# One RWKV-7 mixer layer: pairs' coupling work moved in between the receptance slots, key slots fed two at a time, filler products in the norm's hole

## The chip, the cores and the metric

One Trainium2 chip, one core. The metric is device time of one launch in microseconds, the median of several runs. The kernel runs five engines with queues of their own: TensorE (PE, with weight loads PEld), VectorE (DVE), ScalarE (ACT), GpSimd (POOL) and SyncE (SP, which issues all DMAs here). Each takes its instructions in order and waits at semaphores.

## The reference

One inference step of a 2-layer decoder with d = 1024, for 16 meta + 256 prompt tokens and 8 sequences of 8 new tokens (336 rows together). Each layer is: half an FFN, a token mixer, half an FFN. Layer 0 mixes with RWKV-7 (16 heads of 64), layer 1 with a short gated convolution. The mixer of layer 0, cut to what matters:

```python
xr, xw, xk, xv, xa, xg = [h + xx * mu[c] for c in range(6)]   # xx = previous row - h
r, k, v = xr @ w_rkv[0], xk @ w_rkv[1], xv @ w_rkv[2]
w = -softplus(-(w0 + tanh(xw @ w1) @ w2)) - 0.5
decay = exp(-exp(w))
a = sigmoid(a0 + (xa @ a1) @ a2)
g = sigmoid(xg @ g1) @ g2
kk = k * k_k;  kk = kk / max(norm(kk, per head), 1e-12)
k = k * (1 + (a - 1) * k_a);  b = kk * a
def step(S, inp):
    S = S * d_t + einsum(S, -kk_t) * b_t + v_t * k_t
    return S, einsum(S, r_t)
```

All matrix products are made of three passes of rounded parts (high x high, high x low, low x high), so every weight and every activation is split into a high part (ScalarE) and a low part (VectorE).

## The kernel before, in words

**Weights** come in slots of 1 MB into `raw[0]` and `raw[1]` in turn. `split_act` (L246) writes `w_hi` on ScalarE, `split_dve` (L251) writes `w_lo` on VectorE, and TensorE's use of a slot waits for that. A buffer pair is split anew only when TensorE has ended the slot two earlier. `mix_sp` issues the loads; `load_mix(k)` waits for the split two slots earlier. The stores of z (`couplings`) and their loading back into `gt` follow in the same SP queue.

**The mixer** (`mix_pe`, `mix_act`, `mix_dve`) works on slots in the order: key (0 to 3), decay LoRA (4), a LoRA (5), receptance (6 to 9), gate (10), value (11 to 14), gate out (15). `project` (L811) makes two output tiles of 128 rows per slot, 8 input tiles x 2 x 3 passes = 48 matmuls; a slot with `fresh` waits for each input tile `x_lo` as it arrives. `lora_inner` is L823, `lora_out` L837. Each group of results has PSUM banks given by `BANKS`, and `open_group` waits until these are free.

**The head norm.** ScalarE squares kk, TensorE sums (L846), VectorE takes a max (L1450), ScalarE a root (L1222), VectorE a reciprocal (L1453), and `spread` (L859) spreads the result for each pair of heads.

**The pairs.** For the 8 pairs of heads, VectorE runs `pair_front` (L1546 scan of the log decays, L1549 norm, L1551 and L1553 factors), `pair_back` (L1562, L1566 decays on a, b and k) and `r_decayed` (L1406, which reads the receptance from PSUM). ScalarE makes the exponentials (L1175, L1176, L1184) and, after all pairs, the ends (L1231). TensorE then makes for each pair the couplings (L897, 44 small products), the turned b and k (L883, 44) and the sum for the bonus (L874). VectorE masks the couplings into z (L1492) and makes the product for the sum (L1480); ScalarE keeps the turned rows (L1242, L1243).

**Order written by hand.** Before, TensorE runs two spreads ahead of each receptance slot, and all couplings after the four slots. VectorE runs all fronts and backs first, then a loop over pairs with rk product, `low(XG, p)`, `mixed(XG, p + 4)` and z. After that come the gate slot (10), the value slots, VectorE's triangular inverses (from L1363) and a chain over chunks.

Of the kernel before, what the change touches and what calls it, by code (L numbers as in the profile page):

```python
# [32 lines left out]
P = 128  # L33
# [44 lines left out]
def build_program(nc, x_dram, vec_dram, const_dram, shift_dram, conv_dram, wkv_dram, gu_dram, down_dram,  # L78
                  mix_dram, wo_dram, scin_dram, scout_dram, blockeye_dram, y_out, wkvp_out, wkvs_out, shift_out,
                  convo_out, zt_dram, tt_dram):  # L80
    with ExitStack() as ctx:
# [257 lines left out]

        def ffn_pe(pe, f):  # L340
# [278 lines left out]
        BANKS.update({R_GROUP + i: b for i, b in enumerate((0, 2, 6, 0))})  # L619
# [3 lines left out]
        Z_BANKS = (4, 6)  # L623

        MIXED = {XK: (4, 5, 4, 5), XR: (4, 5, 4, 5), XG: (4, 5, 2, 3), XV: (4, 5, 2, 3)}
# [151 lines left out]
        def mix_pe(pe):  # L777
# [3 lines left out]
            def open_group():  # L781
# [3 lines left out]
                if 2 <= g < R_GROUP + 2:  # L785
                    pe.wait_ge(mix_evac, g - 1)
                elif g == R_GROUP + 3:
                    pe.wait_ge(r_scaled, 2)
                elif g == G_GROUP:
                    pe.wait_ge(kv_turned, PAIRS)  # L790
                elif g == V_GROUP:
                    pe.wait_ge(rk_kept, 1)
                elif V_GROUP < g < GATE_GROUP:
                    pe.wait_ge(mix_evac, g - 5)
                elif g == GATE_GROUP:
                    pe.wait_ge(z_ready, 14)
                elif g > GATE_GROUP:
                    pe.wait_ge(mix_evac, g - 6)
                return BANKS[g]

            def project(slot, ver, fresh, final=False, shift=0):
# [4 lines left out]
                for k in range(KT):  # L806
# [6 lines left out]
                    if final and k < KT - 1:  # L813
                        last.then_inc(x_used, 1)
                last.then_inc(mix_out, 1)
# [25 lines left out]
            for s in range(4):  # L841
                project(s, XK, s == 0, s == 3, PAD)
# [24 lines left out]

            pe.wait_ge(a_normed, PAIRS)

            def sum_rk(p):  # L870
                pe.wait_ge(rk_ready, p + 1)
                if p == 0:
                    pe.wait_ge(r_scaled, PAIRS)
                pe.matmul(PS[0:HEADS, 0, :T], con[:, K_SEL + 16 * p:K_SEL + 16 * p + 16], tmp[p % 2][:, RD],  # L874
                          start=(p == 0), stop=(p == PAIRS - 1)).then_inc(rk_sum, 1)

            def turn_bk(p):
                if p:
                    pe.wait_ge(kv_turned, p)
                for c in range(CHUNKS):  # L880
                    for hh in range(2):
                        rows = slice(HD * hh, HD * hh + HD)
                        last = pe.matmul(PS[rows, 2 + c // 8, (c % 8) * HD:(c % 8 + 1) * HD],  # L883
# [4 lines left out]
            for p in range(PAIRS):  # L888
                pe.wait_ge(a_scaled, p + 1)
                pe.wait_ge(bk_scaled, p + 1)  # L890
                pe.wait_ge(r_scaled, max(p + 1, 6 if p else 1))
                if p >= 2:
                    pe.wait_ge(z_ready, 2 * p - 2)
                for c in range(CHUNKS):
                    for hh in range(2):
                        rows = slice(HD * hh, HD * hh + HD)
                        last = pe.matmul(PS[rows, Z_BANKS[p % 2] + c // 8, (c % 8) * 64:(c % 8) * 64 + 64],  # L897
# [3 lines left out]
                if p >= 1:  # L901
                    turn_bk(p - 1)
                if p >= 2:
                    sum_rk(p - 2)
            turn_bk(PAIRS - 1)
            sum_rk(PAIRS - 2)
            sum_rk(PAIRS - 1)
# [210 lines left out]
        def mix_act(act):  # L1118
# [58 lines left out]

            def decay_r(p):
# [31 lines left out]
            act.activation(thi[:, 1, :], tmp[1][:, :T], ACT.Copy).then_inc(lora_hi, 1)  # L1210
            for s in range(4):
                x_hi_tile(XR, 2 + s)
                evac(6 + s, [(sw[:, m, PAD:], ACT.Sigmoid, vec[:, m, V_W0:V_W0 + 1], False) for m in (2 * s, 2 * s + 1)])
            split(6)
            x_hi_tile(XR, KT - 2)
            x_hi_tile(XR, KT - 1)
            for s in range(4):
                evac(10 + s, [(bk[:, m, :, 0, :], ACT.Sigmoid, vec[:, m, V_A0:V_A0 + 1], True) for m in (2 * s, 2 * s + 1)])
                factors(s)
                if s == 1:  # L1220
                    act.wait_ge(kk_max, 1)
                    act.activation(tmp[3][0:HEADS, :T], tmp[3][0:HEADS, :T], ACT.Sqrt).then_inc(kk_root, 1)  # L1222
            split(7)
            for p in range(PAIRS):
                if p in (2, 4, 6):
                    split(7 + p // 2)
                decay(p)
                if p >= 1:
                    decay_r(p - 1)
# [573 lines left out]
```

## Time and profile before

| | us |
|---|---|
| median of 3 runs | 1461.81 (1461.13 to 1462.18) |
| the profiled execution | 1460.54 |
| its span, first to last instruction | 1458.8 |
| TensorE busy in the span | 1392.3 (95%) |
| VectorE busy | 857.1 (59%) |
| ScalarE busy | 584.8 (40%) |
| mean granted TensorE clock | 0.973 |

The mixer of layer 0 lies between about 266 and 570 us of the span; the part in which the change edits anything ends at about 434. Positions in the rows are microseconds from the start of the span. A row of the timeline merges instructions of one kind that follow each other; its duration is from the first start to the last end, and neighbouring instructions overlap a little, so costs are better read from start to start.

### The profile page before, as it was taken

The numbers are of one execution on the slowest core, as the hardware profiler recorded it, in microseconds if no ns is written. First come the engines' busy times: TensorE is split into PE (matmuls) and PEld (weight loads), VectorE is DVE, ScalarE is ACT, GpSimd is POOL, SyncE is SP. The second block draws the span as 40 slices with busy tenths as digits, with TensorE's granted clock in tenths as the row PEclk, the third lists the DMA queues.
The fourth block names the chain that finished last, engine by engine and source line by source line (L and its number), as shares of the span: only waits on it lengthen the run. The fifth ranks groups of instructions, "written<-read, shape, count | busy, mean of one in ns | idle before, by whom it ended". The sixth has DMA issues, their size and how long they took to land.

```text
span 1458.8 us, 28480 instructions
## 1 busy us (share of the span) xinstructions
PE 1392.3 (95%) x11742; PEld 1350.0 (93%) x11742; DVE 857.1 (59%) x1294; ACT 584.8 (40%) x757; POOL 14.0 (1%) x28
## 2 busy tenths in 40 slices
PE   5999999698799998999999999999999999999997
PEld 5999999686689986899999999999999999999997
DVE  4555544776869366665555555555456867555543
ACT  5333333477344333353333344333333235333332
POOL 0000000300000000000000000000000000000000
PEclk9999999898799899899999999999999999999999
DMA  5333334232125211144443454443444444444342
GB/s 224 130 140 137 135 128 148 103 118 87 59 71 170 73 42 62 58 145 144 144 146 131 145 180 146 145 144 117 148 167 145 145 145 145 144 148 156 126 145 98
DMA packets 44220, 188.98 MB, mean 130 GB/s; under 512 B 15888, under 2 KB 17296, under 8 KB 28016
## 3 DMA queue, kind: packets, MB, share of 16 engines
q1 hardware_dynamic: 44144, 187.89, 37.5%
q8 instruction: 57, 0.93, 0.3%
q14 instruction: 19, 0.16, 0.0%
HBM read 182.65 MB, written 5.22 MB: 129 GB/s over the span
## 4 chain that ended last, share of the span: by engine, by line
PE 90%; DVE 4%; ACT 3%; issue 2%; POOL 1%; DMA 1%; SPq 0%; ACTq 0%; DVEq 0%
PE psum L335 48%; PE psum L367 22%; PE psum L811 5%; PE psum L505 4%; ACT w_hi L246 1%; PE psum L1046 1%; PE psum L997 1%; PE psum L972 1%; PE psum L883 1%; PE psum L1066 1%; DMA w_raw<-in_gu 1%; PE psum L1030 1%; PE psum L897 1%; PE psum L1015 1%; PE psum L1079 1%
## 5 line engine op out<-in xcount | busy, mean ns | idle before, releaser
L251 DVE TENSOR_TENSOR w_lo<-w_raw,w_hi 128x2048 fp32r<-128x2048 f32 (+1 forms) x188 | 388.4, 2066 | 238.4 <-ACT w_hi L246 238.0
L335 PE MATMUL psum<-x_hi,w_hi 128*128 128x322 f32 (+2 forms) x1600 | 499.9, 312 | 19.1 <-DVE x_lo L298 17.5
L246 ACT ACTIVATE w_hi<-w_raw 128x2048 fp32r<-128x2048 f32 (+1 forms) x188 | 326.0, 1734 | 459.0 <-PE psum L335 227.0
L335 PE MATMUL psum<-x_hi,w_lo 128*128 128x322 f32 (+2 forms) x1600 | 500.6, 313 | 0.0
L335 PE MATMUL psum<-x_lo,w_hi 128*128 128x322 f32 (+2 forms) x1600 | 500.5, 313 | 0.0
L335 PEld LDWEIGHTS psum<-x_hi,w_hi 128*128 128x128 f32 x1600 | 303.8, 190 | 20.7 <-issue 17.3
L335 PEld LDWEIGHTS psum<-x_hi,w_lo 128*128 128x128 f32 x1600 | 302.7, 189 | 0.0
L335 PEld LDWEIGHTS psum<-x_lo,w_hi 128*128 128x128 f32 x1600 | 301.8, 189 | 0.3
L367 PE MATMUL psum<-h_hi,w_lo 128*128 128x322 f32 (+2 forms) x704 | 219.8, 312 | 0.0
L367 PE MATMUL psum<-h_lo,w_hi 128*128 128x322 f32 (+2 forms) x704 | 219.2, 311 | 0.0
L367 PE MATMUL psum<-h_hi,w_hi 128*128 128x322 f32 (+2 forms) x704 | 218.8, 311 | 0.0
L367 PEld LDWEIGHTS psum<-h_hi,w_hi 128*128 128x128 f32 x704 | 133.3, 189 | 0.0
L367 PEld LDWEIGHTS psum<-h_hi,w_lo 128*128 128x128 f32 x704 | 132.8, 189 | 0.0
L367 PEld LDWEIGHTS psum<-h_lo,w_hi 128*128 128x128 f32 x704 | 132.5, 188 | 0.0
L390 ACT ACTIVATE h_hi<-tmp 128x322 f32 (+5 forms) x88 | 41.9, 476 | 205.9 <-DVE tmp L434 205.9
L428 DVE TENSOR_TENSOR tmp<-psum,rstd 128x322 f32<-128x322 f32 (+2 forms) x88 | 43.7, 497 | 111.5 <-PE psum L335 106.5
L436 DVE TENSOR_TENSOR h_lo<-tmp,h_hi 128x322 f32 (+5 forms) x88 | 43.8, 498 | 63.8 <-ACT h_hi L390 63.8
L811 PE MATMUL psum<-x_hi,w_hi 128*128 128x336 f32 x208 | 70.4, 339 | 10.5 <-DVE x_lo L1391 10.5
L811 PE MATMUL psum<-x_lo,w_hi 128*128 128x336 f32 x208 | 68.8, 331 | 0.0
L811 PE MATMUL psum<-x_hi,w_lo 128*128 128x336 f32 x208 | 68.5, 329 | 0.0
L278 DVE SCALAR_TENSOR_TENSOR x<-psum,x 128x322 f32<-128x322 f32 (+5 forms) x48 | 23.7, 494 | 72.1 <-PE psum L367 62.3
L811 PEld LDWEIGHTS psum<-x_hi,w_hi 128*128 128x128 f32 x208 | 41.6, 200 | 15.3 <-issue 12.9
(206 smaller groups left out, 1366.1 us busy)
## 6 DMA issues: line engine op xcount, KB each, us to landing
w_raw<-in_gu SPq DMA_DIRECT2D x88, 1024.0 KB, 4.8
w_raw<-in_down SPq DMA_DIRECT2D x64, 704.0 KB, 4.1
w_raw<-in_mix SPq DMA_DIRECT2D x16, 1024.0 KB, 4.8
w_raw<-in_scin SPq DMA_DIRECT2D x12, 1024.0 KB, 4.7
w_raw<-in_wo SPq DMA_DIRECT2D x4, 1024.0 KB, 4.8
w_raw<-in_scout SPq DMA_DIRECT2D x4, 1024.0 KB, 4.8
s<-in_wkv SPq DMA_DIRECT2D x8, 256.0 KB, 3.4
out_wkvs<-s SPq DMA_DIRECT2D x8, 256.0 KB, 2.0
```

Of the source, the lines that this page charges most:

```text
L246: act.activation(whi[par][:, :tiles * P], raw[par][:, :tiles * P], ACT.Copy).then_inc(hi_ready, 1)
L251: dve.tensor_tensor(wlo[par][:, :n], raw[par][:, :n], whi[par][:, :n].bitcast(F32), ALU.subtract).then_inc(lo_ready, 1)
L278: dve.scalar_tensor_tensor(out=x[:, m, c:], in0=ps[:, :T - c], scalar=alpha, in1=x[:, m, c:], op0=ALU.mult, op1=ALU.add).then_inc(x_new, 1)
L335: last = pe.matmul(PS[:, banks[j], :n], w[:, (2 * k + j) * P:(2 * k + j + 1) * P], v[:, k, :n], start=(k == 0 and i == 0), stop=(k == KT - ...
L367: last = pe.matmul(PS[:, 4 + par, :n], w[:, k * P:(k + 1) * P], v[:, kk, :n], start=(kk == 0 and i == 0), stop=(kk == FT - 1 and i == 2))
L390: act.activation(hhi[:, bass.ds(s, 1), :n], tmp[3][:, :n], ACT.Copy).then_inc(hhi_ready, 1)
L428: dve.tensor_tensor(tmp[0][:, :n], PS[:, 2 * par, :n], rstd[:, :n], ALU.mult).then_inc(gate_scaled, 1)
L436: dve.tensor_tensor(hlo[:, bass.ds(s, 1), :n], tmp[3][:, :n], hhi[:, bass.ds(s, 1), :n].bitcast(F32), ALU.subtract).then_inc(hlo_ready, 1)
L505: last = pe.matmul(PS[:, banks[j], :n], w[:, (2 * k + j) * P:(2 * k + j + 1) * P], v[:, k, :n], start=(k == 0 and i == 0), stop=(k == KT - ...
L811: last = pe.matmul(PS[:, b + j, shift:shift + T], w[:, (2 * k + j) * P:(2 * k + j + 1) * P], v[:, k, :], start=(k == 0 and i == 0), stop=( ...
L883: last = pe.matmul(PS[rows, 2 + c // 8, (c % 8) * HD:(c % 8 + 1) * HD], bk[rows, p, c, :, :].rearrange("p h t -> p (h t)"), con[rows, K_EY ...
L897: last = pe.matmul(PS[rows, Z_BANKS[p % 2] + c // 8, (c % 8) * 64:(c % 8) * 64 + 64], bk[rows, p, c, :, :].rearrange("p h t -> p (h t)"), ...
```

## The change

It does the following:

1. After the norm's own product, TensorE issues nine products of constants, 512 columns, into bank 7 (`warm`).
2. Key slots 0 and 1 run together: tile k of slot 0 when it arrives, and tile k - 3 of slot 1 (`pe_tile`).
3. Max, root and reciprocal of the head norm come earlier on VectorE and ScalarE; the banks of the LoRA groups and of the receptance change, and with them the waits in `open_group`.
4. The spreads 2 to 7 stand between the tiles of slot 6; VectorE's norm of a (`a_norm`) is a loop of its own ahead of the pairs.
5. Couplings 0 and 1 and the first sum stand between slots 8 and 9 on TensorE, the other couplings, sums and turns after slot 9 in a new order. VectorE takes z and the rk product inside the loop of pairs. Slot 8 waits for `r_scaled` 2, slot 9 for `r_scaled` 4.
6. ScalarE makes the ends per pair, and does `split(8)`, `(9)`, `(10)` at pairs 1, 3, 5; VectorE too.
7. Gate mixtures use other buffers, and all `low(XG, p)` come after the last z.

```diff
+        def warm(pe, bank, count):
+            for _ in range(count):
+                pe.matmul(PS[:, bank, :], con[:, K_BLOCK:K_BLOCK + P], con[:, 0:512], start=True, stop=True)
+        def pe_tile(pe, par, banks, k, n, xh, xl, shift=0):
+            ...  # the six matmuls of one input tile, as in project
-        BANKS.update({R_GROUP + i: b for i, b in enumerate((0, 2, 6, 0))})
+        BANKS.update({6 + i: b for i, b in enumerate((4, 6, 0, 2, 6, 4, 0, 2))})
+        BANKS.update({R_GROUP + i: b for i, b in enumerate((6, 0, 6, 0))})
-        Z_BANKS = (4, 6)
+        Z_BANKS = (2, 2, 2, 2, 2, 2, 2, 0)
...
-                if 2 <= g < R_GROUP + 2:
+                if 2 <= g < 6:
                     pe.wait_ge(mix_evac, g - 1)
-                elif g == R_GROUP + 3:
-                    pe.wait_ge(r_scaled, 2)
+                elif g == 7:
+                    pe.wait_ge(kk_max, 1)
+                elif 8 <= g < R_GROUP + 2:
+                    pe.wait_ge(mix_evac, (5, 6, 8, 7, 9, 10, 11, 13)[g - 8])
+                elif R_GROUP + 2 <= g < G_GROUP:
+                    pe.wait_ge(r_scaled, 2 * (g - R_GROUP - 1))
                 elif g == G_GROUP:
+                    pe.wait_ge(z_ready, 16)
                     pe.wait_ge(kv_turned, PAIRS)
...
-            for s in range(4):
-                project(s, XK, s == 0, s == 3, PAD)
+            warm(pe, 7, 9)
+            pe_slot_wait(pe, MIXB)
+            banks = [open_group(), open_group()]
+            for step in range(KT + 3):
+                if step < KT:
+                    pe.wait_ge(xlo_ready, 8 * XK + step + 1)
+                    last = pe_tile(pe, 0, (banks[0], banks[0] + 1), step, T, xhi, xlo, PAD)
+                    if step == KT - 1:
+                        last.then_inc(mix_out, 1)
+                if step == 3:
+                    pe_slot_wait(pe, MIXB + 1)
+                if step >= 3:
+                    last = pe_tile(pe, 1, (banks[1], banks[1] + 1), step - 3, T, xhi, xlo, PAD)
+            last.then_inc(mix_out, 1)
+            for s in range(2, 4):
+                project(s, XK, False, s == 3, PAD)
...
+                elif p == 0:                      # in spread(p)
+                    pe.wait_ge(kk_inv, 1)
+                    pe.wait_ge(mix_evac, 12)
-            pe.wait_ge(kk_inv, 1)
-            for s in range(4):
-                spread(2 * s)
-                spread(2 * s + 1)
-                project(6 + s, XR, s == 0, s == 3)
...
+            def couplings(p):
                 pe.wait_ge(a_scaled, p + 1)
                 pe.wait_ge(bk_scaled, p + 1)
-                pe.wait_ge(r_scaled, max(p + 1, 6 if p else 1))
-                if p >= 2:
-                    pe.wait_ge(z_ready, 2 * p - 2)
+                pe.wait_ge(r_scaled, p + 1)
+                if p == 0:
+                    pe.wait_ge(mix_evac, 14)
+                elif p < PAIRS - 1:
+                    pe.wait_ge(z_ready, 2 * p)
+                else:
+                    pe.wait_ge(r_scaled, PAIRS)
...
+            spread(0)
+            spread(1)
+            project(6, XR, True, between=lambda k: spread(k + 2) if k + 2 < PAIRS else None)
+            project(7, XR, False)
+            project(8, XR, False)
+            couplings(0)
+            couplings(1)
+            sum_rk(0)
+            project(9, XR, False, True)
+            couplings(2)
+            sum_rk(1)
+            couplings(3)
+            sum_rk(2)
+            couplings(4)
+            sum_rk(3)
+            turn_bk(0)
+            couplings(5)
+            sum_rk(4)
+            turn_bk(1)
+            turn_bk(2)
+            couplings(6)
+            sum_rk(5)
+            turn_bk(3)
+            turn_bk(4)
+            couplings(7)
+            sum_rk(6)
+            turn_bk(5)
+            turn_bk(6)
+            sum_rk(7)
+            turn_bk(7)
...
             for p in range(PAIRS):                # ScalarE
-                if p in (2, 4, 6):
-                    split(7 + p // 2)
+                if p in (1, 3, 5):
+                    split(8 + p // 2)
                 decay(p)
-                if p >= 1:
-                    decay_r(p - 1)
+                ends(p)
+                decay_r(p)
+            for p in range(3):
+                keep_bk(p)
             x_hi_tile(XG, 0)
             x_hi_tile(XG, 1)
             split(11)
+            keep_bk(3)
+            keep_bk(4)
+            for p in range(5, PAIRS):
+                x_hi_tile(XG, p - 3)
+                keep_bk(p)
...
+            for p in range(PAIRS):                # VectorE
+                a_norm(p)
+                if p == 4:
+                    split(7)
+            dve.wait_ge(mix_evac, 10)
+            dve.wait_ge(bk_padded, 1)
+            for p in range(PAIRS):
+                if p in (1, 3, 5):
+                    split(8 + p // 2)
+                pair_front(dve, p)
+                if p >= 1:
+                    pair_back(dve, p - 1)
+                    r_decayed(p - 1)
+                if p >= 2:
+                    take_z(p - 2)
+                    take_rk(p - 2)
+            pair_back(dve, PAIRS - 1)
+            r_decayed(PAIRS - 1)
+            take_z(PAIRS - 2)
+            take_rk(PAIRS - 2)
+            dve.wait_ge(a_scaled, PAIRS)
+            mixed(XG, 0)
+            mixed(XG, 1)
+            take_z(PAIRS - 1)
+            take_rk(PAIRS - 1)
+            split(11)
+            dve.wait_ge(rk_sum, PAIRS - 1)
+            mixed(XG, 2)
+            dve.wait_ge(rk_sum, PAIRS)
+            mixed(XG, 3)
+            for p in range(PAIRS):
                 low(XG, p)
                 if p + 4 < KT:
                     mixed(XG, p + 4)
```

`take_z(p)` waits for couplings(p) and for the ends of pair p, `take_rk(p)` for the scaled rows of pair p and for the sum two pairs back. `keep_bk(p)` is L1242 and L1243 with their waits. The max and the reciprocal of the head norm move from behind the x_lo tiles of the receptance to ahead of them (max) and to tile 3 (reciprocal); ScalarE's root moves from between the second and third sigmoid group of slot 5 to ahead of the first of slot 4.

## Rows read from the trace of the kernel before

**Rows 1.** The page: its first line and its first section.
```profile
span 1458.8 us, 28480 instructions
PE 1392.3 (95%) x11742; PEld 1350.0 (93%) x11742; DVE 857.1 (59%) x1294; ACT 584.8 (40%) x757; POOL 14.0 (1%) x28
```
**Rows 2.** Windows: stretch, length, busy time of each engine, PEclk, DMA share, GB/s.
```profile
276.60:283.00 6.40, 6.38 (x23) 5.72 (x24) 6.40 (x11) 1.45 (x3) 6.40 (x10) 0.55 0.01 3
...
388.00:400.00 12.00, 7.57 (x132) 7.22 (x132) 11.40 (x24) 5.76 (x11) 0.00 (x0) 0.57 0.01 3
400.00:425.00 25.00, 23.91 (x587) 19.54 (x588) 15.68 (x34) 7.60 (x19) 0.00 (x0) 0.93 0.31 70
```
**Rows 3.** Timeline, key slot 0 on TensorE: start, us, engine, line, operation.
```profile
276.62 0.62 PE L811 MATMUL psum<-x_hi,w_hi 128*128 128x336 f32 x1 [9.55 <-DVE x_lo L1391]
277.03 0.48 PE L811 MATMUL psum<-x_lo,w_hi 128*128 128x336 f32 x1
277.31 0.48 PE L811 MATMUL psum<-x_hi,w_lo 128*128 128x336 f32 x1
...
282.47 0.32 PE L811 MATMUL psum<-x_lo,w_hi 128*128 128x336 f32 x1
```
**Rows 4.** Timeline, VectorE, key tiles and the split behind them.
```profile
275.98 0.49 DVE L1391 TENSOR_TENSOR x_lo<-tmp,x_hi 128x336 fp32r<-128x336 f32 x1
...
277.84 0.49 DVE L1391 TENSOR_TENSOR x_lo<-tmp,x_hi 128x336 fp32r<-128x336 f32 x1
...
286.09 1.14 DVE L1391 TENSOR_TENSOR x_lo<-tmp,x_hi 128x336 fp32r<-128x336 f32 x2
...
291.59 2.29 DVE L251 TENSOR_TENSOR w_lo<-w_raw,w_hi 128x2048 fp32r<-128x2048 f32 x1
```
**Rows 5.** Timeline, ScalarE and VectorE around the root of the head norm.
```profile
335.14 0.98 ACT L1147 ACTIVATE bk<-psum,vec 128x352 f32<-128x352 f32 x2
...
337.42 1.28 ACT L1222 ACT_TABLE_LOAD   x1
...
339.23 2.24 DVE L1453 RECIPROCAL rstd<-tmp 16x336 f32<-16x336 f32 x1 [2.98 <-ACT tmp L1222]
```
**Rows 6.** The chain that ended last, in order of time: start, us, what.
```profile
341.52 2.60 PE psum L859 x4
344.12 9.00 PE psum L811 x48
...
425.72 37.13 PE psum L811 x240
```
**Rows 7.** Timeline, VectorE, pair 2 from its scan to the next pair's.
```profile
358.31 0.85 DVE L1546 TENSOR_TENSOR_SCAN sw<-con,sw 128x336 f32<-128x336 f32 x1
359.20 0.51 DVE L1549 TENSOR_TENSOR ar<-psum,ar 128x336 f32<-128x336 f32 x1
359.62 0.52 DVE L1551 TENSOR_TENSOR bk<-bk,fac 128x352 f32<-128x352 f32 x1
...
360.49 0.62 DVE L1562 TENSOR_TENSOR ar<-ar,tmp 128x15 f32<-128x15 f32 x3
...
361.83 0.85 DVE L1546 TENSOR_TENSOR_SCAN sw<-con,sw 128x336 f32<-128x336 f32 x1
```
**Rows 8.** Timeline, all engines, z and rk of a pair, then one round of the tail.
```profile
399.76 0.95 DVE L1492 TENSOR_TENSOR z<-psum,con 128x512 f32<-128x512 f32 x2
400.63 0.58 DVE L1480 SCALAR_TENSOR_TENSOR tmp<-ar,vec,bk 128x352 f32<-128x352 f32 x1
...
409.13 1.50 PE L897 MATMUL psum<-ar,bk 64*64 64x64 f32 x44
...
410.47 1.45 PE L883 MATMUL psum<-con,bk 64*64 64x64 f32 x44
...
411.85 0.74 PE L874 MATMUL psum<-tmp,con 128*16 128x336 f32 x2
411.96 0.60 ACT L1242 ACTIVATE bk<-psum 128x512 f32<-128x512 f32 x1 [2.19 <-PE psum L883]
```

More of the change, by code:

```diff
@@ L337, in pe_pair @@
             last.then_inc(out_sem, 1)
+        def warm(pe, bank, count):
+            for _ in range(count):
+                pe.matmul(PS[:, bank, :], con[:, K_BLOCK:K_BLOCK + P], con[:, 0:512], start=True, stop=True)
+        def pe_tile(pe, par, banks, k, n, xh, xl, shift=0):
+            for j in range(2):
+                for i, (w, v) in enumerate(passes(whi[par], wlo[par], xh, xl)):
+                    last = pe.matmul(PS[:, banks[j], shift:shift + n], w[:, (2 * k + j) * P:(2 * k + j + 1) * P], v[:, k, :n],
+                                     start=(k == 0 and i == 0), stop=(k == KT - 1 and i == 2))
+            return last
         def ffn_pe(pe, f):
@@ L814, in project @@
                         last.then_inc(x_used, 1)
+                    if between and k < KT - 1:
+                        between(k)
                 last.then_inc(mix_out, 1)
@@ L879, in turn_bk @@
                     pe.wait_ge(kv_turned, p)
+                else:
+                    pe.wait_ge(r_scaled, 6)
                 for c in range(CHUNKS):
@@ L882, in turn_bk @@
                         rows = slice(HD * hh, HD * hh + HD)
-                        last = pe.matmul(PS[rows, 2 + c // 8, (c % 8) * HD:(c % 8 + 1) * HD],
+                        last = pe.matmul(PS[rows, 6 + c // 8, (c % 8) * HD:(c % 8 + 1) * HD],
                                          bk[rows, p, c, :, :].rearrange("p h t -> p (h t)"),
@@ L896, in mix_pe @@
                         rows = slice(HD * hh, HD * hh + HD)
-                        last = pe.matmul(PS[rows, Z_BANKS[p % 2] + c // 8, (c % 8) * 64:(c % 8) * 64 + 64],
+                        last = pe.matmul(PS[rows, Z_BANKS[p] + c // 8, (c % 8) * 64:(c % 8) * 64 + 64],
                                          bk[rows, p, c, :, :].rearrange("p h t -> p (h t)"),
@@ L1454, in mix_dve @@
-            split(7)
-            dve.wait_ge(mix_evac, 14)
-            dve.wait_ge(bk_padded, 1)
-            for p in range(PAIRS):
-                if p in (2, 4, 6):
-                    split(7 + p // 2)
-                pair_front(dve, p)
-                if p:
-                    pair_back(dve, p - 1)
-                if p >= 3:
-                    r_decayed(p - 3)
-            pair_back(dve, PAIRS - 1)
-            dve.wait_ge(a_scaled, PAIRS)
-            r_decayed(PAIRS - 3)
-            for k in range(4):
-                mixed(XG, k)
-                if k % 2:
-                    r_decayed(PAIRS - 2 + k // 2)
@@ L1472, in mix_dve, with a_norm, take_z @@
-            split(11)
-            for p in range(PAIRS):
+            def a_norm(p):
+                dve.wait_ge(kk_spread, p + 1)
+                dve.tensor_tensor(ar[:, 0, p, PAD:], PS[:, 4 + p % 2, :T], ar[:, 0, p, PAD:], ALU.mult).then_inc(a_normed, 1)
+            def take_z(p):
+                dve.wait_ge(z_done, p + 1)
+                dve.wait_ge(ends_ready, 2 * p + 2)
+                for i, (c0, c1) in enumerate(((0, 8), (8, CHUNKS))):
+                    n = (c1 - c0) * 2 * C
+                    dve.tensor_tensor(z[:, :, p, c0:c1, :].rearrange("p h c t -> p c h t"),
+                                      PS[:, Z_BANKS[p] + i, :n].rearrange("p (c h t) -> p c h t", h=2, t=C),
+                                      con[:, K_ZMASK + c0 * 2 * C:K_ZMASK + c1 * 2 * C]
+                                      .rearrange("p (c h t) -> p c h t", h=2, t=C), ALU.mult).then_inc(z_ready, 1)
```

78 lines of the change are left out of this document (30 added, 48 removed).

## The prediction

> **What bounds the kernel now.** The first thing read is the page's head: one core, a span of 1458.8 us [rows 1]. All times below are positions in that profiled execution. The change touches only the mixer of layer 0, so the second view is the chain that ended last, in order of time. From 425.72 it is one unbroken stretch of TensorE work, 240 matmuls in 37.13 us (the G slot and the four V slots; 0.155 us a matmul, so 7.4 us a slot of 48) [rows 6]. TensorE goes on almost without a hole after that. What comes behind the start of the G slot is not edited, so the change is worth what it does to that one start, 425.72.
>
> Ahead of it, the windows and the timeline show TensorE waiting often, with its clock at half (1.2 GHz) for long parts: 0.55 granted in 276.6 to 283, 0.57 in 388 to 400 [rows 2]. The hole of the norm is 9.55 us long [rows 3]. In the pairs' stretch VectorE is the busiest (11.40 of 12 us in 388 to 400); in 400 to 425 TensorE is busy 23.91 of 25 [rows 2]. So before, VectorE does the eight pairs first, and then TensorE runs couplings, turns and sums pair by pair.
>
> **The change, part 1: the filler in the norm's hole.** Nine products of 512 columns with plain f32 operands. No row has this shape. Two f32 products of 336 columns took 2.60 us at half clock [rows 6], so 1.3 each with the drain, 0.65 at full clock, and 512/336 times that is 1.0: nine are 9 us, from 267.1 to 276.1, before the first key tile starts at 276.62 [rows 3]. At half clock they would take 17.8 us and end at 284.9; that bound costs 5.6 us below. TensorE was at full clock as the hole began, so I take the first.
>
> What does it buy? The first matmuls after the hole repeat every 0.28 us, and from 282.47 a matmul takes 0.32 from start to end, at full clock [rows 3]. But a tile of six at half clock is 1.7 us, and tiles arrive every 1.87 (275.98, 277.84) [rows 4], so half speed is hidden by VectorE. The row says 0 for the filler. The Trainium skill (TensorE: Matmul & The Clock Gate, Why this matters for your kernels) advises to warm TensorE up with matmuls ahead of the work. By that rule the forecast would be 1480.6; it stands among the rivals.
>
> **Part 2: two key slots per arriving tile.** Tile 7 of x_lo is ready at 287.2 (286.09 + 1.14) [rows 4]. Three tiles of slot 0 are done by 282.1; then 13 tiles remain (5 of slot 0, 8 of slot 1) at 0.93, so both end at 294.1. Before, slot 0 ends at 288.8 and slot 1 at 296.2: 2.1 us saved. But slot 0 now ends at 290.5, and its end frees the buffer for the split of slot 2: ScalarE 1.9, then VectorE 2.2 (2.29 recorded [rows 4]), ready at 294.8. So 0.7 goes back into a wait, and **1.4 us** remain. At the filler's bad bound the 16 tiles run from 284.9 to 299.8 instead.
>
> **Part 3: the root moved ahead.** Before, ScalarE does the square root between two pairs of sigmoids: a table load of 1.28 from 337.42, the root of 0.5 (VectorE starts behind it at 339.23), a table load again, then VectorE's reciprocal of 2.24, and at 341.52 the first spread [rows 5, 6]. After, the root stands ahead of all sigmoids (one load of 1.28 less in all), and the reciprocal is inside the receptance's x_lo loop, off the end. The spread now waits for bank 4, for the evacuation of group 11, which ended at 336.12 before (335.14 + 0.98) [rows 5]. From there: -1.4 (part 2), +1.8 (root and its load now ahead of it), +1.2 (ScalarE waits for receptance tile 5, which stands behind the reciprocal on VectorE), +0.5 (tiles 6 and 7 ahead of split 6): 338.2. The receptance starts **3.3 us earlier**.
>
> **Part 4: spreads between tiles.** The same eight spreads, six of them now inside slot 6. TensorE starts at half clock as before (slot 6 took 9.00 instead of 7.4 [rows 6]). Walking tile by tile, slot 6 with all spreads ends at 353.15, slot 7 at 360.55. VectorE is only free of the last spread at 352.0, since a_norm(p) can only follow spread p.
>
> **Part 5: the pairs, where the time is decided.** VectorE's costs from start to start [rows 7]: split 2.2; pair_front without the norm 1.75 (scan 0.89, then 360.49 - 359.62 = 0.87); pair_back 1.34 (361.83 - 360.49); r_decayed 0.42, taken from the norm of a, which also multiplies 128x336 out of PSUM (359.62 - 359.20). A z pair is 0.88, an rk product 0.50 [rows 8]. Two new waits bind them:
> - slot 8 uses the banks of slot 6 and waits for r_scaled 2; slot 9 uses those of slot 7 and waits for r_scaled 4;
> - VectorE goes on from r_decayed(1) straight into take_z(0), whose couplings stand behind slot 8 on TensorE; and from r_decayed(3) into take_z(2), behind slot 9.
>
> So each slot waits for VectorE, and VectorE waits for each slot; queued behind that wait are splits 9 and 10 and all later pairs. From 352.0: front 0 to 353.75; ScalarE does three exponentials, two small ones and split 8 by 356.85; VectorE's split to 359.05; two fronts, two backs, two r (7.0) to 366.05. TensorE idles 5.5 us; slot 8 runs to 373.45 and couplings 0 (1.5) to 374.95: **8.9 us of idle VectorE**. Then z, rk, split 9, front, back, r, z, rk, front, back, r: 2 x 1.38 + 2.2 + 2 x 3.51 = 12.0, to 386.95. Slot 9 ends at 394.35 (385.8 before), with VectorE idle 8.9 again.
>
> The tail begins there (S). Before, it was paced by TensorE at 3.38 a pair: couplings at 409.13, turn at 410.47, sum at 411.85 (1.34, 1.38, 0.66) [rows 8]. After, couplings 1 to 6 share one bank pair, so each waits for the z before it. The chain: VectorE from S+1.5 to the factor product of pair 7 is 3 x 1.38 + 2.2 + 2 x 3.51 + 1.31, S+16.2; ScalarE's last decays 1.55; keep_bk 0.87 (0.60 + 0.32 recorded [rows 8]), turn, keep, turn, couplings 6 to S+23.85; z 6, rk 6, two mixtures, x_hi, ScalarE's split 11 (1.9), keep 3 to S+29.4; turn 4, couplings 7, z 7, rk 7, VectorE's split 11 to S+35.9; mixture 2, x_hi, keep 5, turn 6, sum 7 to S+39.9; mixture 3, x_hi, keep 6, turn 7, keep 7: **S+44.0**, against 39.9 before. G may start at 438.4 instead of 425.7: **+12.7 us** with TensorE at full clock throughout.
>
> **Part 6: the clock.** A restart after a hole cost 2.85 us at 276.62 (half speed to 282.47) [rows 3] and 1.6 in slot 6 [rows 6]. Slots 8 and 9 now restart after 5.5 and some 8 us: bounds 1.6 and 2.9, I take 2.5 each, nearer the long hole. In the tail nine TensorE steps of 1.45 are on the chain; at half clock each costs about 1.1 more. Before, the thinly filled stretch from 388 stood at 0.57 and the dense one after 400 at 0.93 [rows 2], so bounds 0 and 10; I take 3. G's own start: 0 to 2.9, I take 1.
>
> **Sum:** 12.7 + 5.0 + 3 + 1 = 21.7. On the profiled span 1480.5; this execution was timed 1460.5 and the median of the runs is 1461.8, so **1483.5**. The stores of z, the loads and the inverses keep their slack: they end some 2 us after G's start where VectorE asks for them 14 us after it, so I count 0.
>
> **Rivals.**
> - **Real overlap, faster.** If TensorE never waited from 338.2, it needs 4 x 7.4 + 8 x 0.66 + 8 x 3.38 = 62 us and G starts at 400: 1436. Half of that gain is 1449. It decides where r_decayed(1) comes before slot 7 ends (360.6). For it: VectorE is busy only 857 of 1459 us over the kernel. Against: a split's stall and 12 us of work stand between 352.0 and that point, and take_z(0) is behind slot 8 whatever comes. Chance 0.06.
> - **VectorE-bound, but the tail's ring doesn't bite.** The two holes of 8.9 us remain; the tail overlaps and G starts when VectorE is through its own work, at about 428: 1464, from 1461 to 1469. Chance 0.07, of which 0.03 are within 0.2%.
> - **The filler overruns** (half clock): 5.6 us more, 1489. It is inside the range. Chance 0.07.
> - **The filler saves time.** If the key slots were bound by TensorE and not by the arriving tiles, full speed from 276.6 on would save half of the 5.85 us spent at half clock, 2.9 us: 1480.6. The gaps of 0.1 to 0.2 us between tiles already at half clock speak against it. Chance 0.03. (This is what the Trainium skill's advice above amounts to.)
> - **All bad bounds of the clock together:** 12.7 + 5.8 + 10 + 2.9 = 31.4, 1493. Chance 0.08.
> - The forecast, serial slots and tail, +13 to +27: 0.69.
>
> **How the numbers follow.** The range: 1472 as the forecast with no loss of clock, less 3 for my tile-by-tile positions, gives 1470 (rounded up); at the top 1493. The first two rivals stay mostly outside it, with part of the last. A difference under 0.2% (2.9 us) can't be told from none. Faster 0.06, same 0.03, slower 0.91.
>
> **What would show it.** Right: in the window from 352 to 400 VectorE has two idle times of 9 to 12 us ahead of a z row, released by psum of the couplings; TensorE has holes ahead of slots 8 and 9, released by r_decayed; G starts near 445; the key slots end 1.4 us earlier. Wrong: G before 428, or slots 7, 8 and 9 back to back. If the filler matters, the first key tiles run at 0.155 a matmul and yet the key slots end no earlier, as VectorE feeds them.

## The result, and the profile after

| kernel | median us | lowest to highest, runs | ratio to before, 95% interval |
|---|---|---|---|
| before | 1461.47 | 1459.09 to 1462.18, 4 | |
| changed | 1497.74 | 1495.55 to 1498.86, 4 | 1.0249 [1.0232, 1.0267] |

The changed kernel is slower by 36.3 us. The prediction had the sign and the place right, but the time lies 14.2 us above its value and above the range's top of 1493. The profiled execution took 1498.86 us with a span of 1497.1, against 1458.8 [rows 1]: 38.3 us more where 21.7 were predicted.

The page's head, its first section and the clock:

```profile
span 1497.1 us, 28542 instructions
...
PE 1417.3 (95%) x11760; PEld 1366.1 (91%) x11760; DVE 857.4 (57%) x1294; ACT 584.0 (39%) x770; POOL 14.0 (1%) x28
```

VectorE and ScalarE are busy for the same time as before [rows 1]; TensorE is busy 25 us longer. The nine filler products are 7.9 us of that (266.88 to 274.77, in a hole where TensorE was idle before); the rest is nearly the same matmuls running slower. So part of the loss is TensorE running slower, and the rest is waiting. The chain of waits in order of time (start, us, what; the longest pieces) shows where:

```profile
291.93 1.93 ACT w_hi L246
...
293.88 2.30 DVE w_lo L251
...
296.23 15.04 PE psum L829 x96
...
339.95 2.57 PE psum L896 x4
342.52 1.98 PE psum L829 x6
344.50 1.41 PE psum L896 x2
345.91 1.98 PE psum L829 x6
...
362.88 3.67 PE psum L829 x12
366.64 1.93 ACT w_hi L246
...
378.06 10.17 PE psum L829 x48
388.23 1.45 PE psum L932 x44
...
401.90 10.20 PE psum L829 x48
412.10 1.45 PE psum L932 x44
...
459.74 39.83 PE psum L829 x240
...
630.96 31.18 PE psum L517 x192
```

Against [rows 6], the first spread starts 1.6 us earlier (339.95 for 341.52), and the G slot starts 34.0 us later (459.74 for 425.72). Everything in between is the receptance, the pairs and the tail. The windows (columns as in [rows 2]) give TensorE's clock there:

```profile
277.00:283.00 6.00, 5.39 (x20) 4.63 (x20) 6.00 (x10) 1.45 (x3) 6.00 (x10) 0.57 0.01 3
283.00:289.00 6.00, 6.00 (x36) 6.00 (x35) 5.62 (x16) 1.46 (x3) 2.54 (x6) 0.86 0.01 1
...
342.00:366.00 24.00, 24.00 (x60) 15.90 (x60) 7.48 (x11) 7.64 (x15) 0.00 (x0) 0.50 0.18 65
388.00:400.00 12.00, 3.83 (x92) 2.86 (x90) 10.22 (x20) 1.85 (x7) 0.00 (x0) 0.89 0.25 89
...
459.70:470.00 10.30, 10.26 (x49) 10.29 (x50) 8.69 (x18) 4.61 (x11) 0.00 (x0) 0.71 0.04 15
```

The third line is the surprise: all of slot 6 with its spreads, 24 us, was granted 0.50, the lower level (1.2 GHz), although TensorE was never idle in it. The fourth shows TensorE at work for 3.83 of 12 us; before, it was 7.57 [rows 2].

Two views show the mutual wait of part 5. First the waits from 340 to 470 (engine, line, released by: us in total, times, longest), then VectorE's timeline:

```profile
DVE z L1533 <- PE psum L932: 33.2, 4, 11.8
...
PE psum L829 <- DVE ar L1474: 13.0, 2, 8.9
```
```profile
389.70 0.96 DVE L1533 TENSOR_TENSOR z<-psum,con 128x512 f32<-128x512 f32 x2 [11.79 <-PE psum L932]
...
401.25 0.50 DVE L1474 TENSOR_TENSOR ar<-psum,tmp 128x336 f32<-128x336 f32 x1
413.57 0.96 DVE L1533 TENSOR_TENSOR z<-psum,con 128x512 f32<-128x512 f32 x2 [11.82 <-PE psum L932]
```

VectorE idles 11.79 us ahead of the z of pair 0 and 11.82 ahead of that of pair 2. Each time it waits for couplings that stand behind a slot on TensorE (slots 8 and 9), and each of these slots had waited for VectorE (4.03 and 8.93 us). From the z at 389.70 to the end of r_decayed(3) at 401.75, where slot 9 is released, are 12.05 us.

### The profile page after: what moved, and what is told of

It is laid out like the page before. It is cut to its first block, busy times and chain, and to the rows that moved or that the text cites. A ratio compares the mean times of both kernels' runs of the same rounds, so it can differ in the third digit from the quotient of the medians.

```text
span 1497.1 us, 28542 instructions
## 1 busy us (share of the span) xinstructions
PE 1417.3 (95%) x11760; PEld 1366.1 (91%) x11760; DVE 857.4 (57%) x1294; ACT 584.0 (39%) x770; POOL 14.0 (1%) x28
## 4 chain that ended last, share of the span: by engine, by line
PE 90%; DVE 5%; ACT 3%; issue 2%; DMA 1%; POOL 0%; SPq 0%; DVEq 0%; ACTq 0%
PE psum L335 47%; PE psum L379 21%; PE psum L829 6%; PE psum L517 4%; DVE w_lo L251 1%; PE psum L348 1%; PE psum L1105 1%; ACT w_hi L246 1%; PE psum L1056 1%; PE psum L896 1%; PE psum L1031 1%; PE psum L914 1%; PE psum L1125 1%; DMA w_raw<-in_gu 1%; PE psum L1089 1%
## 5 line engine op out<-in xcount | busy, mean ns | idle before, releaser
L335 PEld LDWEIGHTS psum<-x_hi,w_hi 128*128 128x128 f32 x1600 | 303.7, 190 | 21.2 <-issue 17.3
L829 PE MATMUL psum<-x_hi,w_hi 128*128 128x336 f32 x176 | 63.7, 362 | 14.8 <-DVE ar L1474 13.0
L829 PE MATMUL psum<-x_lo,w_hi 128*128 128x336 f32 x176 | 61.7, 351 | 0.0
L829 PE MATMUL psum<-x_hi,w_lo 128*128 128x336 f32 x176 | 61.3, 348 | 0.0
L829 PEld LDWEIGHTS psum<-x_hi,w_hi 128*128 128x128 f32 x176 | 38.1, 217 | 22.5 <-issue 21.5
```

The costliest lines, as they stand in the source:

```text
L335: last = pe.matmul(PS[:, banks[j], :n], w[:, (2 * k + j) * P:(2 * k + j + 1) * P], v[:, k, :n], start=(k == 0 and i == 0), stop=(k == KT - ...
L829: last = pe.matmul(PS[:, b + j, shift:shift + T], w[:, (2 * k + j) * P:(2 * k + j + 1) * P], v[:, k, :], start=(k == 0 and i == 0), stop=( ...
```

## Experiments

Every difference to the changed kernel below is one of medians. The kernel before, timed beside each of these runs, came to 1460.8 to 1461.8, so a difference of about 1 us says nothing.

**The mutual wait: couplings ahead of their slot.** If VectorE's idle time comes from couplings queued behind slots 8 and 9, moving one pair's couplings ahead of each slot must give most of it back.

```diff
-            project(8, XR, False)
             couplings(0)
+            project(8, XR, False)
             couplings(1)
             sum_rk(0)
-            project(9, XR, False, True)
             couplings(2)
+            project(9, XR, False, True)
```

> The changed kernel with one reordering on TensorE alone: couplings 0 ahead of slot 8 instead of behind it, couplings 2 ahead of slot 9. Theory (VectorE stands still at take_z behind the slot): the two idle times of 11.8 us ahead of a z row shrink to under 4 us, slot 9 starts about 7 us earlier after slot 8's start (16.6 instead of 23.8), VectorE is another 7 us ahead at the end of slot 9, and the time falls by 12 to 16 us, to about 1484. Rival (TensorE's slots at half clock set the pace, VectorE's waits are only their shadow): the waits move elsewhere and the time falls by less than 4 us.

Measured: 1480.5 us (1479.22 to 1484.25, 4 runs), 1.0141 [1.0121, 1.016] of before, 17.2 less than the changed kernel. The waits of the same stretch, then the chain:

```profile
DVE z L1533 <- PE psum L932: 16.8, 4, 8.1
```
```profile
377.12 7.62 PE psum L829 x48
...
391.33 9.18 PE psum L829 x48
```

The waits for z fall from 33.2 to 16.8 us. Slot 9 starts 14.2 us after slot 8, where the changed kernel has 23.8 between them. The gain is more than the expected 12 to 16 us, although a wait of 8.1 us for a z stays, in the tail. The matmuls and VectorE's work are the same. This mechanism is shown, and no other single edit gave back as much.

Not all of it is waiting saved directly. In the two profiles the G slot starts 16.6 us earlier (443.12). Of this, 7.1 is less waiting between the slots, 3.6 is slots 8 and 9 running faster (7.62 and 9.18 us for 10.17 and 10.20; slot 8 was granted 1.00 here and 0.72 in the changed kernel), 5.0 is a shorter tail, and 0.9 lies ahead of the edit.

**The spreads out of slot 6.** Four spreads ahead of the slot and four behind it, so that nothing stands between its tiles.

```diff
-            spread(0)
-            spread(1)
-            project(6, XR, True, between=lambda k: spread(k + 2) if k + 2 < PAIRS else None)
+            for p in range(4):
+                spread(p)
+            project(6, XR, True)
+            for p in range(4, PAIRS):
+                spread(p)
...
-                if p == 4:
+                if p == 3:
                     split(7)
```

> The changed kernel with the spreads taken out from between the tiles of slot 6: spreads 0 to 3 ahead of slot 6, 4 to 7 behind it, and VectorE's split 7 one pair earlier so that nothing waits for it. Theory (the spreads between the tiles are what held TensorE at half clock from 340 to 367): the clock returns some 6 us into the receptance, slot 6 takes 9 to 10.5 us without spreads and slot 7 ends near 366 instead of 374; the time falls by 7 to 10 us, to about 1489. Rival (TensorE would have stayed at half clock in this stretch anyway, because it began there): slot 6 runs at 0.28 us a matmul to its end, slot 7 ends at 372 or later, and the time falls by at most 3 us.

Measured: 1490.21 us (1486.61 to 1491.9, 4 runs), 1.019 [1.0172, 1.0209], 7.5 less than changed. Chain, then windows:

```profile
339.73 4.81 PE psum L896 x8
344.54 9.71 PE psum L829 x48
```
```profile
342.00:350.00 8.00, 8.00 (x27) 6.54 (x27) 3.72 (x4) 6.22 (x10) 0.00 (x0) 0.55 0.32 111
350.00:366.00 16.00, 14.56 (x84) 12.60 (x82) 7.53 (x11) 3.40 (x7) 0.00 (x0) 1.00 0.12 40
```

Slot 6 alone takes 9.71 us, with the clock back at 1.00 from 350. In the changed kernel it was still at 0.50 at 366. This is what the theory expected (7 to 10 us).

**The same order, spreads of 128 rows.** A spread multiplies 16 rows of the inverse norms (16 heads) with a constant. This kernel contracts over all 128 rows instead, in the changed kernel's order; the further rows add nothing to the product.

```diff
-                pe.matmul(PS[:, 4 + p % 2, :T], con[0:HEADS, K_SELT + P * p:K_SELT + P * p + P], rstd[0:HEADS, :],
+                pe.matmul(PS[:, 4 + p % 2, :T], con[:, K_SELT + P * p:K_SELT + P * p + P], rstd[:, :],
```

> The changed kernel with each spread contracting over all 128 rows instead of 16 (the weights of the other rows are zero, so the result is the same; order, count, columns and types unchanged). Theory A (what keeps TensorE at half clock is that the spread uses 16 of the 128 rows): the granted clock returns to full within about 6 us of the start of slot 6, slot 6 with its spreads takes 14 to 16 us instead of 24.6, and the time falls by 8 to 12 us. Theory B (it is the waits between tile and spread, or f32 products as such, or zero weights don't count): slot 6 stays at half clock and the time is the same within 2 us.

Measured: 1485.4 us (1484.59 to 1487.12, 4 runs), 1.0167 [1.015, 1.0184], 12.3 less than changed. Windows, then two rounds on TensorE:

```profile
342.00:346.00 4.00, 4.00 (x16) 3.44 (x14) 0.61 (x2) 3.93 (x8) 0.00 (x0) 0.62 0.07 31
346.00:352.00 6.00, 6.00 (x34) 5.21 (x32) 4.05 (x5) 1.54 (x2) 0.00 (x0) 1.00 0.15 20
```
```profile
349.97 0.73 PE L896 MATMUL psum<-rstd,con 128*128 128x336 f32 x2
350.28 0.57 PE L829 MATMUL psum<-x_hi,w_hi 128*128 128x336 f32 x1
...
351.46 0.45 PE L896 MATMUL psum<-rstd,con 128*128 128x336 f32 x1
```

The clock is at 1.00 from 346, and a round (a spread and a tile of six) takes 1.49 us, 349.97 to 351.46. In the changed kernel a round takes 3.39 (342.52 to 345.91). Same instructions, same order: the number of rows decides. Slot 7 ends at 361.4 here and at 374.0 in the changed kernel. The gain is just above the expected 8 to 12 us. The slow mixture isn't an accident of one execution: from the first spread to the last two tiles it takes 22.9 us in the changed kernel (339.95 to 362.88), and 22.9 again in the profiles of the kernels with couplings first and without filler.

**Full clock ahead of the receptance.** Does a mixture of tiles and 16-row products pull the clock down, or does it only fail to raise it? Four filler products stand ahead of the first spread here, once its bank is about to be free.

```diff
+            pe.wait_ge(mix_evac, 11)
+            warm(pe, 7, 4)
             spread(0)
             spread(1)
```

> The changed kernel with four more filler products (f32, 512 columns, 128 rows, bank 7) on TensorE ahead of spread 0; the 16-row spreads stay between the tiles of slot 6. The dense value slots with 16-row products kept full clock, so the theory is now: that mixture keeps a full clock and only fails to raise a half one. Then, with the clock raised by the four products (from 337.8 to about 344.6, which delays the first spread by some 4.7 us), slot 6 runs at full clock with rounds of 1.9 us instead of 3.4, ends near 361 instead of 367, and the time falls by 4 to 8 us. Rival (in this stretch the mixture, with its short waits for VectorE, pulls the clock down again): slot 6 is back at half clock within its first tiles and the time is 2 to 5 us above the changed kernel's.

Measured: 1489.46 us (1488.41 to 1493.44, 4 runs), 1.0199 [1.018, 1.0219], 8.3 less than changed. Window, then two rounds:

```profile
342.00:354.00 12.00, 12.00 (x52) 7.76 (x52) 5.66 (x8) 5.36 (x9) 0.00 (x0) 1.00 0.13 36
```
```profile
350.02 0.83 PE L896 MATMUL psum<-rstd,con 16*128 16x336 f32 x2
350.78 0.42 PE L829 MATMUL psum<-x_hi,w_hi 128*128 128x336 f32 x1
...
351.91 0.55 PE L896 MATMUL psum<-rstd,con 16*128 16x336 f32 x1
```

The same mixture, entered at full clock, keeps it, and the gain is just above the expected 4 to 8 us. A round takes 1.89 us (350.02 to 351.91), 0.4 more than with 128 rows. So the loss of part 4 has two terms: a clock that does not come back, and a dearer product.

**The same question in a dense stretch of the kernel before.** Fourteen extra products between the tiles of two value slots, of 16 rows in one kernel and 128 in the other; both also wait for the last z ahead of the value slots (the expectation says that nothing else is changed, but this wait is added too, alike in both).

```diff
+                    if extra and k < KT - 1:
+                        pe.matmul(PS[:, 7, :T], con[0:HEADS, K_SELT:K_SELT + P], con[0:HEADS, 0:T], start=True, stop=True)
...
+            pe.wait_ge(z_ready, 16)
             for s in range(4):
-                project(11 + s, XV, s == 0)
+                project(11 + s, XV, s == 0, extra=s in (1, 2))
```

> The kernel before with one more product behind each of the first seven tiles of value slots 12 and 13: f32, 336 columns, contracting over 16 rows, into bank 7, which nothing reads (14 products added, nothing else changed). TensorE is dense and at full clock there. Theory (a mixture of tiles and 16-row products is by itself enough to pull the clock down): the granted clock falls to 0.5 inside slot 12 and stays there to the end of slot 13; the two slots take about 40 to 48 us instead of 15, the time rises by 25 to 33 us. Rival (such products only fail to raise a clock that is already low): the clock stays at 1.00 and the time rises by 14 x 0.7 = 10 us.

> The same 14 added products in value slots 12 and 13, contracting over all 128 rows. Theory (rows are what matters): the clock stays at 1.00 and the time rises by about 10 us (14 x 0.7). Rival (f32 products as such pull the clock down): it falls as with 16 rows and the time rises by 25 us or more.

Measured, one run each: 1476.68 us with 16 rows (15.4 above before's 1461.27) and 1469.4 with 128 (8.1 above). The 16-row kernel's window, then one round of it and one with 128 rows:

```profile
442.00:468.00 26.00, 26.00 (x116) 17.22 (x114) 16.03 (x53) 5.19 (x6) 0.00 (x0) 1.00 0.33 114
```
```profile
442.81 0.83 PE L816 MATMUL psum<-con 16*128 16x336 f32 x2
...
444.69 0.83 PE L816 MATMUL psum<-con 16*128 16x336 f32 x2
```
```profile
441.92 0.72 PE L816 MATMUL psum<-con 128*128 128x336 f32 x2
...
443.40 0.73 PE L816 MATMUL psum<-con 128*128 128x336 f32 x2
```

The clock stays at 1.00 from 442 to 468 in both kernels, so my theory that such a mixture lowers it is wrong. What remains is the price: rounds of 1.88 and 1.48 us, 0.4 us a product or some 5.5 us over 14. The two times differ by 7.3 us, and single runs don't tell what the other 1.8 are; 0.8 of them are there at the start of the G slot (426.99 for 426.18), ahead of the products.

**128-row spreads in the kernel before**, where the spreads stand together.

```diff
-                pe.matmul(PS[:, 4 + p % 2, :T], con[0:HEADS, K_SELT + P * p:K_SELT + P * p + P], rstd[0:HEADS, :],
+                pe.matmul(PS[:, 4 + p % 2, :T], con[:, K_SELT + P * p:K_SELT + P * p + P], rstd[:, :],
```

> The kernel before with its eight spreads contracting over all 128 rows (zero weights in the other 112). Theory (16-row products let the clock fall or hold it low): the half-clock stretches behind the spreads of slots 8 and 9 (364 to 367, 378 to 381) get shorter or vanish; but VectorE and ScalarE pace that part, so the gain is 0 to 4 us. Rival (those falls come from the idle times of 1.9 us alone): the granted clock of the stretches is as before, within 0.05, and the time is the same.

Measured: 1461.55 us (1459.67 to 1463.62, 10 runs), 1.0001 [0.9991, 1.0011]: nothing. This doesn't show that the form costs nothing there. From the start of the pair of spreads between slots 6 and 7 to the second matmul behind it are 1.58 us with 16 rows (353.04 to 354.62) and 1.29 with 128 (353.50 to 354.79). But VectorE and ScalarE set the pace of that part, so TensorE's gain buys no time. In one of the two stretches that the expectation names the clock did differ (1.00 instead of 0.54 in 364 to 367), in the other it didn't (0.50 in 378 to 381); with one profile each, what it owes to the rows stays open.

**The filler taken out.**

```diff
-            warm(pe, 7, 9)
             pe_slot_wait(pe, MIXB)
```

> The changed kernel without the nine filler products. Theory (half clock is hidden behind VectorE's pace of the key tiles in any case, and with the filler the clock fell anyway at 278): within 1.5 us of the changed kernel, the key slots 0 and 1 ending between 294 and 296. Rival (the filler is worth what it keeps warm): 2.5 us or more slower than with it.

Measured: 1494.21 us (1492.78 to 1495.95, 4 runs), 1.0223 [1.0206, 1.024]: 3.5 less than with it, more than the 1.5 us of the theory and the other way than the rival. Its windows:

```profile
277.00:283.00 6.00, 6.00 (x23) 5.33 (x23) 6.00 (x10) 1.45 (x3) 6.00 (x10) 0.56 0.01 3
283.00:289.00 6.00, 6.00 (x41) 6.00 (x40) 5.62 (x16) 1.46 (x3) 2.58 (x6) 1.00 0.00 0
```

Without the filler the clock is back at 1.00 for all of 283 to 289; with it that window has 0.86. In the changed kernel's profile the filler kept the clock up through the hole, but once the paced tiles came the clock fell all the same. The first tile's matmuls repeat every 0.155 us, those of the second at half speed. TensorE's timeline there:

```profile
276.82 0.31 PE L348 MATMUL psum<-x_lo,w_hi 128*128 128x336 f32 x1
276.97 0.32 PE L348 MATMUL psum<-x_hi,w_lo 128*128 128x336 f32 x1
...
278.81 0.48 PE L348 MATMUL psum<-x_lo,w_hi 128*128 128x336 f32 x1
279.09 0.48 PE L348 MATMUL psum<-x_hi,w_lo 128*128 128x336 f32 x1
```

But this fall is not the same in every execution. The 128-row kernel has the same filler and the same code up to here, and its profile shows the full clock throughout:

```profile
276.60:283.00 6.40, 4.28 (x23) 3.47 (x23) 6.40 (x12) 1.56 (x4) 6.40 (x11) 1.00 0.00 0
```

So does the warmed kernel's. Slot 2 starts at 296.23 in the changed kernel, but at 295.14 to 296.00 in the four other profiled kernels with the filler (295.25 with 128-row spreads), and at 295.13 to 295.33 in the three without it. A clock held at full through the paced tiles thus brought slot 2 no earlier than no filler at all: the filler saves no time here. That it costs 3.5 us is not shown. At the G slot the two profiles differ by 2.1 us (457.65 for 459.74): 1.1 from the key slots, where kernels with the filler differ as much among themselves, and 1.0 from slot 8 (9.18 for 10.17 us), which starts some 100 us behind the filler. What makes this 1.0, and the rest of the 3.5, isn't settled.

The Trainium skill (TensorE: Matmul & The Clock Gate, Why this matters for your kernels) advises to keep TensorE busy for full throughput and, so that a matmul is measured accurately (the row behind the prediction's sentence), to warm it up with matmuls first. Four products ahead of the receptance, where dense work follows, were worth 8.3 us here, and nine ahead of tiles that VectorE feeds were worth nothing. Being busy was not enough in slot 6: TensorE was busy for all 24 us from 342 to 366 and was granted 0.50.

**All of it together, and a version that beats both.** Starting from the changed kernel: no filler, 128-row spreads, the couplings of pairs 0 and 2 ahead of slots 8 and 9 and those of 1 and 3 inside them, ScalarE's split 8 one pair earlier, more bk kept before split 11 on ScalarE, two x_lo tiles and two mixtures ahead of split 11 on VectorE, one load on SP later. The core of it on TensorE:

```diff
-            warm(pe, 7, 9)
...
-            project(8, XR, False)
             couplings(0)
-            couplings(1)
+            project(8, XR, False, between=lambda k: couplings(1) if k == 1 else None)
             sum_rk(0)
-            project(9, XR, False, True)
             couplings(2)
+            project(9, XR, False, True, between=lambda k: couplings(3) if k == 1 else None)
             sum_rk(1)
-            couplings(3)
             sum_rk(2)
```

> The changed kernel with its causes of loss taken away together: no filler; spreads over 128 rows; couplings 0 ahead of slot 8, couplings 1 and 3 inside slots 8 and 9 behind their second tile, couplings 2 between them; split 8 ahead of pair 0's exponentials on ScalarE; ScalarE keeps all turned rows ahead of gate tiles 2 to 7 and does split 11 between keep 6 and keep 7; SyncE's load 13 behind all stores of z. Theory (VectorE's own work of about 4.9 us a pair is then the bound): the receptance's slots end near 385, the gate slot starts between 405 and 415 (425.7 before, 459.7 in the changed kernel), and the time is 1442 to 1455, faster than the kernel before. Rival (the tail's chain of turn, keep and sum stays in force, or the clock falls again in the gaps): the gate slot starts at 425 or later and the time is 1461 or more.

Measured: 1453.78 us (1451.19 to 1456.5, 5 runs), 0.9951 [0.9934, 0.9967]: faster than before. Waits of 340 to 470 and the start of the G slot:

```profile
DVE z L1528 <- PE psum L931: 6.4, 3, 3.4
```
```profile
416.33 0.40 PE L829 MATMUL psum<-x_hi,w_hi 128*128 128x336 f32 x1 [1.21 <-ACT bk L1295]
```

VectorE's waits for z are down to 6.4 us, and the G slot starts 9.4 us earlier than before [rows 6]. The time is inside the expected 1442 to 1455, the start of the G slot 1.3 us behind the expected 405 to 415. The edits were made together, so how much each gives in this kernel isn't known. At the wo slot, 586.83 for 593.50, 6.7 are left. Behind 416.33 the chain that ended last now runs through VectorE's mixtures, x_lo tiles and splits, no longer through one stretch of matmuls, and so 2.7 us go back.

A second step puts the sum of pair 1 inside slot 9 and split 11 before keep 5 on ScalarE and before mixture 3 on VectorE:

```diff
-            project(9, XR, False, True, between=lambda k: couplings(3) if k == 1 else None)
-            sum_rk(1)
+            project(9, XR, False, True, between=lambda k: couplings(3) if k == 1 else sum_rk(1) if k == 3 else None)
```

> The overlapped kernel (e8) with sum 1 inside slot 9 behind its fourth tile instead of behind the slot, and split 11 ahead of keep 5 on ScalarE and ahead of mixture 3 on VectorE. Theory (VectorE waits 2.3 us for sum 1, and the gate slot's start waits for keep 7, which stands behind split 11): the gate slot starts at 412 to 415 instead of 416.3 and the time falls by 1 to 4 us, to 1450 to 1453. Rival (turns and keeps in turn set the tail whatever stands between them): within 1 us of e8's 1453.8.

Measured: 1450.82 us (1448.41 to 1453.83, 4 runs), 0.9921 [0.9904, 0.9937], the best here. But the G slot starts at 416.75, outside what was expected, and the two profiled spans are equal (1451.9 and 1452.0). So the step didn't do what it was meant to. The runs of the two kernels overlap widely, and whether the 3 us between the medians are a difference at all stays open.

## Why the prediction was right or wrong

**Parts 1 and 2** (filler 0, key slots −1.4): the nine products took 7.9 us where 9 was said and didn't overrun, and their worth was rightly taken as nothing. The 1.4 us didn't come in this execution. VectorE's and ScalarE's splits took what was said, but slot 0 freed its buffer at 291.9 and not at 290.5, as the tiles run slow until 284.5. Slot 2 starts at 296.23, where it did before. In six of the seven other kernels with these key slots it starts at 295.1 to 295.3, so some 1 us of the 1.4 is usual and the profiled execution missed it by chance.

**Part 3** (root): predicted 338.2, measured 339.95 (339.0 where slot 2 started earlier); the 1.4 of part 2 are missing, and 0.35 more. A step too small, but right in kind.

**Part 4, the step that failed.** I let slot 6 run "at half clock as before", that is with a restart of 1.6 us, and walked it to 353.15 for slot 6 and 360.55 for slot 7. Slot 7 ended at 374.03. The sizes of a spread and the time for which half clock lasts were taken from spreads standing together and from a slot without them [rows 6]; the trace of before had no row for the mixture, and I set no bound for it, though I did set bounds for the clock everywhere else. Less the late start, this term was 11.7 us too small: most of the miss. The 128-row kernel and the warmed one give back 12.3 and 8.3 us, which confirms size and place. In the 128-row kernel the first spread starts 0.8 us later than predicted (338.98) and slot 7 ends at 361.4, against 360.55 walked, and slot 8 waits 5.42 us against 5.5: the walk was sound but for what the 16-row products do between tiles. A bound of half clock over all of slot 6 (eight tiles at 1.68 us, eight spreads at 1.3 from [rows 6]) would have ended the slot near 362.0 instead of 353.15, most of the way to the 364.9 that it comes to less the late start; the rest is that such a product between tiles costs more than 1.3.

**Part 5** held. Predicted: two idle times of VectorE of 8.9 plus 2.5 for the clock, measured 11.79 and 11.82; 12.0 of work between, measured 12.05; slot 8 waits 5.5, measured 4.03; tail of 44.0 plus 3, measured 47.7 (412.03 to 459.74). Moving the couplings ahead of the slots took 17.2 us away, some 3.6 of it by a faster clock in the slots, so the reason is tested and not only the numbers. That the sum over this part came out near is in part luck: the loss of 3 us of clock in the tail was taken between bounds of 0 and 10.

**Part 6**: slots 8 and 9 take 10.17 and 10.20 where 7.4 + 2.5 was said. The G slot took 10.29 and its stretch of 240 matmuls 39.83 instead of 37.13 [rows 6], 2.7 where I took 1 from bounds of 0 and 2.9: the upper bound was the nearer one. The wo slot takes 31.18 us, 1.1 more than before. Its code is the same in all twelve profiled kernels, and it takes 30.0 to 31.5 in them, so this can't be put down to the change.

**The sum.** 38.3 − 21.7 = 16.6: start of the receptance 1.75, slot 6 11.7, slots 8 and 9 −0.8, tail 0.7, clock of the G slot 1.7, and 1.6 behind it (0.7 up to the wo slot, 0.9 in it and after). One figure of the prediction is wrong in itself: the forecast with no loss of clock is 1461.8 + 12.7 = 1474.5 and not 1472, so the range's lower end was 2.5 us too low. The miss is at the other end.

**The rivals.** Real overlap at 1436 to 1449 didn't happen, since take_z(0) stood behind slot 8, as the argument against it said. With that order mended, and the filler and the 16-row spreads gone, the same idea does gain, though less than the 13 to 26 us of the rival: 7.7 and 10.6. The tail's ring was there (47.7 us), the filler neither overran its hole nor saved time, and the bad bounds of the clock together (1493) still lacked the one that mattered.

## What to carry to other kernels

When work is interleaved on two engines that each run in order, follow both queues at once: an engine waiting for a short result that stands behind a long slot on the other stops everything queued behind that wait, and if the slot in turn waits for that engine, both idle in turns. Put the short piece that the other engine wants ahead of the long one: that alone took 17.2 of the 36 us of loss away here, and with the other edits the loss became a gain of 8 to 11. And where an edit mixes forms of matmul that never stood side by side in the trace, take the half clock over the whole stretch as a bound, not the length of an earlier restart. And before a difference of 1 us is put down to an edit, look at the same stretch in another kernel whose code there is the same.

## What the runs showed of the hardware

- Tiles of six 128-row matmuls with a 16-row f32 product between them, entered at half clock, stayed at 0.50 for 24 us with TensorE never idle; entered at full clock the same mixture stayed at 1.00 (342 to 354 with four products ahead of it, 442 to 468 in the dense stretch). With 128 rows, in the same order and from the same half clock, it came back to 1.00 by 346. The runs show that the rows decide; what in the chip makes it so they don't show.
- An f32 product of 336 columns and 16 rows between such tiles costs about 0.95 us at full clock and about 1.7 at half; with 128 rows it costs about 0.56 and 1.1. These are rounds of 1.89, 3.39, 1.49 and 2.80 us (the last from 340.87 to 343.67 in the 128-row kernel), less a tile of 0.93 at full clock or 1.68 at half. So fewer rows were the dearer form. With two such products side by side between slots the difference was smaller, some 0.3 us for the pair at full clock, and the time was the same (ratio 1.0001), as other engines set the pace there.
- The clock differed between executions where the code did not: with the same filler, the key tiles of 276.6 to 283 were granted 0.57, 0.60, 0.73, 1.00 and 1.00 in five kernels.
